# A hybrid attention and RWKV step: the second branch's values made token by token, and scores issued ahead of the preceding turn

## The reference

```
gates, aq, ak, av, bq, bk, bv, cin = _split(h @ p['w_in'], IN_SPLITS)
...
out_a = map_query_blocks(lambda q: _gqa_block(q, keys_a, vals_a), rope(qa))
...
def _diff_block(q1, q2, k1, k2, v, lam):
    s1 = einsum('bhqd,bhkd->bhqk', q1, k1) * sc
    s2 = einsum('bhqd,bhkd->bhqk', q2, k2) * sc
    p = softmax(s1) - lam * softmax(s2)
    return einsum('bhqk,bhkd->bhqd', p, v)
```

## Time and profile before

| | us |
|---|---|
| median of three runs | 2612.16 |
| the runs | 2609.24, 2612.16, 2616.32 |
| the profiled execution | 2606.47 |
| its span, first to last instruction | 2604.6 |
| PE busy | 2451.4 (94% of the span) |
| DVE busy | 1376.4 (53%) |
| ACT busy | 1050.4 (40%) |
| POOL busy | 321.4 (12%) |

### The profile page before, as it was taken

How to read it: one execution, slowest core, us unless ns; L and a number is a source line. 1 busy time by engine, 2 the same in 40 slices (tenths; PEclk the granted TensorE clock), 3 DMA queues, 4 the chain that set the end, 5 groups by cost and what they waited for, 6 DMA issues and landing times. The chain is left out here.

```text
span 2604.6 us, 57653 instructions
## 1 busy us (share of the span) xinstructions
PE 2451.4 (94%) x23806; PEld 2297.3 (88%) x23806; DVE 1376.4 (53%) x2306; ACT 1050.4 (40%) x1705; POOL 321.4 (12%) x312
## 2 busy tenths in 40 slices
PE   5999999999989889999979999999999899999998
PEld 3989989889978889999968999998899788899997
DVE  2433355576487655443354344655765775644434
ACT  3333244355644335332253332434555342343323
POOL 0000032000033303000100001310001341220001
PEclk7999999999999999999989999999999999999999
DMA  7875634333300023446467755333332001334373
GB/s 265 253 231 178 212 97 133 87 87 90 101 8 4 28 64 103 127 125 204 122 205 227 231 180 176 101 112 90 90 91 74 4 4 30 106 100 129 112 225 110
DMA packets 482190, 320.02 MB, mean 123 GB/s; under 512 B 15474, under 2 KB 438920, under 8 KB 481800
## 3 DMA queue, kind: packets, MB, share of 16 engines
q1 hardware_dynamic: 481928, 316.32, 40.4%
HBM read 311.30 MB, written 4.98 MB: 121 GB/s over the span
## 5 line engine op out<-in xcount | busy, mean ns | idle before, releaser
L855 PE MATMUL acc<-xm_hi,w_hi 128*128 128x384 f32 x2352 | 808.0, 344 | 38.0 <-DVE xm_lo L2208 33.8
L2198 DVE TENSOR_TENSOR w_lo<-raw,w_hi 128x1024 fp32r<-128x1024 f32 (+1 forms) x420 | 521.5, 1242 | 517.0 <-ACT w_hi L1625 508.9
L857 PE MATMUL acc<-xm_hi,w_lo 128*128 128x384 f32 x2352 | 793.8, 338 | 0.0
L856 PE MATMUL acc<-xm_lo,w_hi 128*128 128x384 f32 x2320 | 783.4, 338 | 0.0
L1625 ACT ACTIVATE w_hi<-raw 128x1024 fp32r<-128x1024 f32 (+1 forms) x420 | 439.6, 1047 | 299.1 <-PE acc L857 167.0
L855 PEld LDWEIGHTS acc<-xm_hi,w_hi 128*128 128x128 f32 x2352 | 448.1, 191 | 63.8 <-issue 34.8
L857 PEld LDWEIGHTS acc<-xm_hi,w_lo 128*128 128x128 f32 x2352 | 447.6, 190 | 0.0
L856 PEld LDWEIGHTS acc<-xm_lo,w_hi 128*128 128x128 f32 x2320 | 442.1, 191 | 0.5
L855 PE MATMUL acc<-h_hi,w_hi 128*128 128x384 f32 x704 | 242.1, 344 | 7.8 <-DVE w_lo L2198 7.8
L856 PE MATMUL acc<-h_lo,w_hi 128*128 128x384 f32 x704 | 239.7, 340 | 0.0
L857 PE MATMUL acc<-h_hi,w_lo 128*128 128x384 f32 x704 | 239.6, 340 | 0.0
(11 more groups left out here) (368 smaller groups left out, 3445.7 us busy)
## 6 DMA issues: line engine op xcount, KB each, us to landing
raw<-in_ffn_w_in SPq DMA_DIRECT2D x179, 512.0 KB, 4.0
modw<-in_w_mod SPq DMA_DIRECT2D x71, 1024.0 KB, 6.0
raw<-in_w_in SPq DMA_DIRECT2D x114, 512.0 KB, 4.2
raw<-in_ffn_w_out SPq DMA_DIRECT2D x64, 512.0 KB, 4.3
raw<-in_ffn_w_out SPq DMA_DIRECT2D x32, 384.0 KB, 3.2
raw<-in_w_up SPq DMA_DIRECT2D x24, 512.0 KB, 3.6
modx<-in_w_mod SPq DMA_DIRECT2D x9, 1024.0 KB, 11.7
raw<-in_w_out SPq DMA_DIRECT2D x16, 512.0 KB, 3.7
```

Of the source, the lines that this page charges most:

```text
L855: pe.matmul(out, lhs[0], rhs[0], start=first, stop=False)
L856: pe.matmul(out, lhs[0], rhs[1], start=False, stop=False)
L857: return pe.matmul(out, lhs[1], rhs[0], start=False, stop=last)
L2198: done(dve.tensor_tensor(w_lo[:, c % SPL, 0:w], raw[:, c % RAW, 0:w], w_hi[:, c % SPL, 0:w].bitcast(F32), ALU.subtract), lo_done)
```

## The change

The second branch's values are made with tokens on the partitions at once. The stationary operand is now a block of 128 tokens (`xm_hi`, `xm_lo`), the moving operand the weights, 512 columns wide. A value chunk is therefore another piece of `w_in`: 256 features by all 512 columns, in runs of 2 KB where it was 1024 features by 128 columns. The four chunks add up in three banks, one for each block of tokens, which stay open over units 0 to 3; a fourth bank is passed over so that the ring of banks comes out even. DVE copies the three to `vb` at the end of unit 3, the last in two halves, of which one frees the bank passed over. The turns of these values, their copies to `gu` and back, and the waits between them are gone; the first branch's values keep theirs. Second, each unit's `scores` stand ahead of the `turn` of the unit before.

```diff
@@ plan_fillers
     for i in range(NB):
         fill[i].append(("bv", i))
-        fill[i + 1].insert(0, ("vt", i + 1))
@@ plan_layer
+            elif key[0] == "bv":
+                chunks.append(key)
+                if key[1] == 0:
+                    groups.extend(("bvt", c) for c in range(NCH + 1))
@@ chunk_src
+                if kind == "bv":
+                    r0 = key[1] * 256
+                    return lay("w_in")[:, r0:r0 + 256, COL_BV:COL_BV + 512].rearrange("l (k p) c -> p (l k) c", p=128), 2, 512
@@ PE
+                    def values(i, half):
+
+                        key = ("bv", i)
+                        open_chunk(key)
+                        if i == 0:
+                            for c in range(NCH):
+                                open_group(("bvt", c))
+                        for k in (2 * i, 2 * i + 1):
+                            if half is not None and k % 2 == 1:
+                                half()
+                            s, col = chunk_no[key] % SPL, k % 2 * 512
+                            wide = w_hi[:, s, col:col + 512], w_lo[:, s, col:col + 512]
+                            for c in range(NCH):
+                                hi, lo = xm_tile(k, slice(c * 128, (c + 1) * 128))
+                                out = gbank(("bvt", c))[:, :]
+                                pe.matmul(out, hi, wide[0], start=k == 0, stop=False)
+                                pe.matmul(out, hi, wide[1], start=False, stop=False)
+                                mm = pe.matmul(out, lo, wide[0], start=False, stop=k == KD - 1)
+                        mm.then_inc(chunk_used, 1)
...
-                        elif key[0] == "vt":
-                            turn_values(key[1])
+                        elif key[0] == "bv":
+                            values(key[1], half)
...
                     for u, un in enumerate(units):
+                        scores(un)
                         if u >= 1:
                             turn(units[u - 1])
-                        scores(un)
@@ DVE
+                    def take_values():
+
+                        for c in range(NCH):
+                            key = ("bvt", c)
+                            wait_group(dve, key)
+                            if c < NCH - 1:
+                                freed(dve.tensor_copy(vb[:, c, :], gbank(key)[:, :]), key)
+                            else:
+                                skipped = ("bvt", NCH)
+                                dve.wait_ge(free_sem(skipped), group_no[skipped] // ACC)
+                                freed(dve.tensor_copy(vb[:, c, 0:256], gbank(key)[:, 0:256]), skipped)
+                                freed(dve.tensor_copy(vb[:, c, 256:512], gbank(key)[:, 256:512]), key)
...
-                            if key[0] == "bv":
-                                take_values(key[1] + 1)
-                            elif key[0] == "vt":
-                                take_turned(key[1])
+                            if key == ("bv", NB - 1):
+                                take_values()
```

More of the change, by code:

```diff
@@ L58 @@
 B_QK = [(kind, i) for kind in ("bq", "bk") for i in range(4)]
-V_KEYS = [("av", 0)] + [("bv", i) for i in range(4)]
 ACC = 4
@@ L199, in plan_layer @@
         if g[0] in ("rot", "vt", "shift"):
+            continue
+        if g[0] == "bvt":
+            last[g] = chunk_no[("bv", NB - 1)]
             continue
@@ L777, in _ @@
                         load_chunk(chunk_list[n])
-                    for n in range(NB + 1):
-                        wait_freed(sy, ("vt", n))
+                    wait_freed(sy, ("vt", 0))
+                    for c in range(NCH):
+                        wait_freed(sy, ("bvt", c))
                     sy.dma_start(O["new_attn_v_l"][bass.ds(l, 1)].rearrange("l h p d -> p (l h) d"),
@@ L1060, in _ @@
                             mm.then_inc(kt_done, 1)
-                    turn_values(0)
+                    turn_values()
                     def rotate(i, bank):
@@ L1151, in weigh @@
                         if tile == NB and un["first"]:
-                            wait_freed(pe, ("vt", NB))
+                            for g in range(NCH):
+                                wait_freed(pe, ("bvt", g))
                         if un["first"] and tile > NB:
@@ L1201, in _ @@
                         for key in fillers[u]:
-                            if second is not None and key[0] not in ("rot", "vt"):
+                            if second is not None and key[0] != "rot":
                                 filler(key, lambda: turn(units[u - 1], 1))
@@ L1793, in _ @@
                         for key in fillers[u]:
-                            if key[0] not in ("rot", "vt"):
+                            if key[0] != "rot":
                                 ahead(key)
@@ L2325, in _, with take_turned @@
                         ahead(key)
[L2327 to L2337, removed]
-                        freed(dve.tensor_copy(dst, gbank(key)[:, 0:TOK].rearrange("p (c v) -> p c v", c=NCH)), key)
+                    def take_turned():
+                        dve.wait_ge(vt_done, 1)
+                        key = ("vt", 0)
+                        freed(dve.tensor_copy(va[:, 0:NCH, :], gbank(key)[:, 0:TOK].rearrange("p (c v) -> p c v", c=NCH)), key)
+                    def take_values():
+                        for c in range(NCH):
+                            key = ("bvt", c)
[7 more added lines that the diff above has]
+                                freed(dve.tensor_copy(vb[:, c, 256:512], gbank(key)[:, 256:512]), key)
                     ahead(("av", 0))
                     dve.wait_ge(cmix_ready, C_BLOCKS)
-                    take_values(0)
+                    wait_group(dve, ("av", 0))
+                    freed(dve.tensor_copy(gu[:, 0, :], gbank(("av", 0))[:, 0:TOK]), ("av", 0))
                     dve.wait_ge(rms_std, 1)
```

12 lines of the change are left out of this document (6 added, 6 removed).

## The result

| | median, us | lowest to highest | profiled execution | its span |
|---|---|---|---|---|
| before | 2607.72 (6 runs) | 2600.62 to 2616.32 | 2606.47 | 2604.6 |
| changed | 2589.59 (6 runs) | 2584.17 to 2594.09 | 2588.95 | 2587.0 |

The ratio of changed to before is 0.9933, 95% interval 0.9915 to 0.9951: 17.5 us less, 13 to 22 by the interval. The forecast was 11.7 us less, 2600.5, range 2592 to 2609.

The account below looks back on a forecast made before the run. The prediction took TensorE's queue, busy 94% of the span, as the bound. Its terms, 2.4 + 1.2 + 0.6 + 4.9 + 2.6 = 11.7 us, came off a 2612.2 us median to give 2600.5 us, range 2592 to 2609.

Parts of the forecast that it names:

- Turns of values and their wait: Units 1 to 4: removed transposes save 1.2 us per layer, the wait before unit 1's another 0.61 us.
- the projection: Second-branch values: 72 matmuls of 512 columns replace 96 of 384, saving 0.3 us per layer, 0.6 for two.
- my constant of 13.3 ns: Projection: each matmul's surplus over streaming time assumed the same at 512 columns, giving 226.7 ns each.
- The waits for the normalised tile: Units 17, 20, 23: scores ahead of the turn remove a wait of 0.82 us each, 4.9 us for two layers.
- The change of shape: Other units: reordering saves part of an array reshaping, 0.12 us for 11 units, 2.6 us for two layers.
- rival 2: Projection and units: weight load hidden and a whole shape change saved, 15.7 us less, 2596.5 us; chance 0.07.
- a hidden weight load: Projection: 512 columns hide the 13.3 ns load, 213.3 ns per matmul, worth 1.3 us per layer.
- the load shapes: Weight loads for the values: new shape with 2 KB runs costs nothing, as no wait there is for a load.
- the exponentials: ACT's exponentials may come 0.86 us later after the reordering; unit 17 showed 1.6 us of slack.
- Rival 3: All units: the softmax chain becomes the bound, costing 39.6 us less the 11.7, 2640 us; chance 0.06.
- DVE's block of copies: End of unit 3: four copies, at most 2.8 us, cost nothing under 3.05 us of cover before unit 5's scores.
- The sum: Whole kernel: terms of 2.4, 1.2, 0.6, 4.9 and 2.6 us for two layers total 11.7 us.

Follow-up runs that it names:

- the second timing: The unmodified changed kernel timed once more against the kernel before: ratio 0.993 (0.9914 to 0.9945).
- values_only: The changed kernel with the turn put back in front of the scores, values still token by token: 0.997 of before, 7.8 us less.
- +192: The changed kernel with 48 tiny matmuls (192 instructions) in PE's idle time ahead of the second stage; 12.9 us slower than the changed kernel by the ratios.
- order_only: The kernel before with scores ahead of the turn in every unit, values still row by row with their turns: 0.9976 of before, 6.3 us less.
- dense_run: The kernel before with 384 more 64x64 matmuls in one run ahead of unit 0 in each layer: 2653.08 us in one run.

## Why the prediction was right, and where it was wrong

- **Turns of values and their wait** (1.2 + 0.6 us per layer) and **the projection** (0.3): 2.1 forecast, 2.1 measured by the units. The total fits better than the term of the projection: at 230 ns in the mean, 72 matmuls take 16.6 us as the 96 did, so it is worth some 0.1 us rather than the 0.3 of my constant of 13.3 ns. By the Trainium skill ("TensorE: Matmul & The Clock Gate", "Wait — 56ns, not 53.3ns?") 512 columns would take some 216 ns; that is an estimate from its formula, and the rows say 230.
- **The waits for the normalised tile**: 0.82 each forecast, 0.88 measured, 2.65 us per layer.
- **The change of shape** was mis-sized: 0.12 us for 11 units, 1.3; units 2 to 11 gained 0.15 to 0.22 each, 1.8, and unit 12 lost 0.06, because its scores now wait 0.21 us for DVE. (The streaming of rows 8 adds up to 1.38 us and not 1.35, so a change is 0.20 us.) I had taken the middle between no and a whole change; it is nearly the whole. The turn in mid-projection, which has no change around it, pointed there, and my discount had no row. By the Trainium skill ("TensorEngine Tiling (Array Packing)", "Key Properties"), where "Mode switching requires drain", the saved change counts in full, and the measurement is near that. This is the one half of rival 2 that came; its other half, a hidden weight load, did not.
- **Costed at nothing**: the load shapes and the exponentials cost nothing. Rival 3, slower, did not occur in a single unit: no scores wait for ACT. DVE's block of copies did not touch unit 5, where I looked, and which went from 6.84 to 6.67 like its neighbours. It did cost unit 4 what the order would have brought there, by the 0.16 us for which its weighing waits: cover was counted up to the next scores, and the weighing comes before them. (The block also replaces two copies in unit 3, not one.)
- **The sum was of the units alone**: 11.7 forecast, 13.1 measured there. The step that failed is this one: I listed what the change does to the waits and the work of the units and took the rest of the program to be unmoved. But in each layer it also takes 77 instructions from PE's stream ahead of the chain (36 matmuls with their weight loads, and 5 separate waits), and the blocks of 256 then end elsewhere in it. The 17.5 us are 4.4 more than the units give, and the 17.9 of both timings are 4.8 more. The lower end of the first interval, 13, would leave nothing over; the second timing's, 14, hardly anything. What the block ends are worth is 7.4 us in the chain by the two profiles, 3.6 us by the timed `values_only` less its 4.2, and 2.8 and 7.2 by the changed kernel with the ends moved back. So they account for the rest or most of it, to within a few us. The profile of before had the row, 14.7 us of issue waits in the chain, the second of PE's list, and the prediction never spoke of it.
- **Luck**: nothing in the change aims at the block ends. That they came to lie at the best of the five places tried is chance; at +192 the same change gains 5.0 us in all.
- **The base**: the forecast counted from a median of three runs, 2612.2, and the six runs gave 2607.7. That is 4.4 of the 10.9 us between forecast and result; 1.4 are the terms of the units; the other 5.1 are what had no term, mostly the chain. From the median of six the same sum gives 2596.0, and a range with the same distances reaches down to 2587.5, below the result: with the right base, the missing chain would not have put the time outside.

Open stays why the next block's transfer starts early in a block in some places and at its very end in others, why moving the ends alone gave the kernel before so much less than its profiles show, and why `order_only` gained less than its units.

## What to carry to other kernels

Where PE runs through straight code in bursts of small matmuls, look at its waits for issue and count its instructions ahead of them: an edit upstream can move these waits. Here that cost the changed kernel 0.1 to 0.5% of its time by the place, at the worst place as much as the units had gained. Such a shift looks like a gain or a loss of the edit; tiny matmuls in an idle stretch told the two apart here. And compare unit by unit, start to start: there 0.04 us can be read where whole runs scatter by 10.

## What the hardware showed that I had not expected

- PE's instructions come in 16 KB transfers of 256, one fp32 64 x 64 matmul being four of them. At 14.6 ns each a run of 1536 did not stall; the chain's bursts between waits did where a block ends, up to 4.1 us (in `dense_run`).
- In a row of empty waits that are already satisfied, each takes PE 104 ns (18.6 us for 179); an instruction of a tiny matmul takes a seventh of it.
- A stretch of 3.4 us at half the clock costs the units stage 0.9 to 1.7 us, and it falls in or out of it from one execution to the next.
